# A transformer trunk on one core: layer 0's feed-forward with the context tokens in a pass of their own and the latents' up projection as seven block products

## The reference

```python
def _conv_ffn(u, w_up, conv_w, w_down):
    gate, val = jnp.split(_dwconv3(u @ w_up, conv_w), 2, axis=-1)
    return (jax.nn.silu(gate) * val) @ w_down

for layer in range(DEPTH):            # DEPTH = 2
    mod = silu(c) @ ada_w[layer] + ada_b[layer]      # 6 parts of 1024; mod_c the same from c_ctx
    ...                                              # the layer's mixer, h = h + gt1 * y
    h = h + gt2 * _conv_ffn(_modulate(_rmsnorm(h, norm2[layer]), sh2, sc2), *ffn)
    if not last:
        hc = hc + cgt2 * _conv_ffn(_modulate(_rmsnorm(hc, norm2[layer]), csh2, csc2), *ffn)
```

## Time and profile before

| | |
|---|---|
| median of 3 runs | 3210.61 us (3210.31 to 3213.64) |
| the profiled execution | 3206.37 us, of which the span shown in the trace is 3204.4 us |
| PE busy | 3016.6 us (94%) |
| DVE busy | 1765.9 us (55%) |
| POOL busy | 1015.6 us (32%) |
| ACT busy | 953.6 us (30%) |
| mean granted TensorE clock | 0.974 of full speed |

### The profile page before, as it was taken

One profiled execution on the slowest core, in us unless ns is written; L12 is line 12 of the kernel. 1 busy time (PEld: TensorE's weight loads), 2 busy tenths in 40 slices (PEclk: granted clock), 3 DMA queues, 4 the chain that ended last, 5 costly groups with the idle time before them and its releaser, 6 DMA issues. The chain is left out here.

```text
span 3204.4 us, 67073 instructions
## 1 busy us (share of the span) xinstructions
PE 3016.6 (94%) x28758; PEld 2470.4 (77%) x28758; DVE 1765.9 (55%) x2673; ACT 953.6 (30%) x1800; POOL 1015.6 (32%) x644
## 2 busy tenths in 40 slices
PE   6998999999999999899989889999988899999999
PEld 4655888888888888788867667878767678888887
DVE  4623444555554454722246666777755766666666
ACT  4011221000000000220036566666632433233232
POOL 3212223223333323152311100000004466666664
PEclk9998999999999999999989989999989999999999
DMA  5431011222222221022312011111012111111112
GB/s 236 151 123 37 23 46 46 86 92 92 92 92 92 80 85 40 20 89 81 99 47 63 21 33 29 31 32 34 23 40 92 38 42 66 40 53 66 40 53 79
DMA packets 86541, 210.55 MB, mean 66 GB/s; under 512 B 8434, under 2 KB 44658, under 8 KB 86003
## 3 DMA queue, kind: packets, MB, share of 16 engines
q1 hardware_dynamic: 73442, 157.21, 14.7%
q10 hardware_dynamic: 12816, 49.16, 4.4%
HBM read 185.50 MB, written 20.84 MB: 64 GB/s over the span
## 5 line engine op out<-in xcount | busy, mean ns | idle before, releaser
L155 POOL TENSOR_TENSOR w_hi<-w_raw,zero 128x1024 fp32r<-128x1024 f32 x93 | 177.9, 1913 | 830.0 <-PE ps L167 552.7
L167 PE MATMUL ps<-u_hi,w_hi 128*128 128x512 f32 (+1 forms) x1560 | 395.1, 361 | 3.3 <-DVE ffn_cv L869 2.2
L167 PE MATMUL ps<-u_lo,w_hi 128*128 128x512 f32 (+1 forms) x1560 | 391.4, 358 | 0.0
L167 PE MATMUL ps<-u_hi,w_lo 128*128 128x512 f32 (+1 forms) x1560 | 391.4, 358 | 0.0
L167 PEld LDWEIGHTS ps<-u_hi,w_hi 128*128 128x128 f32 x1560 | 259.6, 188 | 74.2 <-issue 26.6
L167 PEld LDWEIGHTS ps<-u_hi,w_lo 128*128 128x128 f32 x1560 | 259.9, 188 | 46.5
L167 PEld LDWEIGHTS ps<-u_lo,w_hi 128*128 128x128 f32 x1560 | 259.8, 188 | 46.4
L1318 ACT ACTIVATE ffn_cv<-ps,small 128x1280 f32<-128x1280 f32 x44 | 58.6, 1332 | 688.8 <-PE ps L167 680.3
L867 DVE SCALAR_TENSOR_TENSOR ffn_cv<-ps,small,ffn_cv 128x1023 f32<-128x1023 f32 x88 | 77.7, 883 | 307.9 <-ACT ffn_cv L1318 306.4
L158 POOL TENSOR_TENSOR w_lo<-w_raw,w_hi 128x1024 fp32r<-128x1024 f32 x93 | 228.3, 2455 | 7.3
L1697 POOL TENSOR_TENSOR f_w_lo<-h,f_w_hi 128x512 fp32r<-128x512 f32 x92 | 138.4, 1514 | 149.7 <-ACT f_w_hi L1905 149.7
(11 more groups left out here) (443 smaller groups left out, 7040.0 us busy)
## 6 DMA issues: line engine op xcount, KB each, us to landing
w_raw<-in_ffn SPq DMA_DIRECT2D x66, 512.0 KB, 3.4
ada_tile<-in_ada_rows ACTq DMA_DIRECT2D x64, 512.0 KB, 4.0
h<-in_ffn SPq DMA_DIRECT2D x34, 512.0 KB, 4.8
f_w_raw<-in_ffn SPq DMA_DIRECT2D x32, 512.0 KB, 4.0
ada_ring_s<-in_ada SPq DMA_DIRECT2D x22, 512.0 KB, 3.3
w_raw<-in_cd_in SPq DMA_DIRECT2D x20, 512.0 KB, 4.2
z_scratch<-cd_stage ACTq DMA_DIRECT2D x15, 640.0 KB, 5.5
ada_first<-in_ada SPq DMA_DIRECT2D x16, 512.0 KB, 15.5
```

The lines of the kernel that those rows point to most:

```text
L155: pool.tensor_tensor(hi, K.raw[:, raw, :], K.zero[:, 0:1].to_broadcast([P, KT * P]), ALU.add).then_inc(self.hi_done, 1)
L167: mm = pe.matmul(K.ps[:, slot, c, 0:width], wt[:, s, w], x[:, k, at:at + width], start=start and n == 0, stop=stop and n == 2)
```

## The change

`ffn_phase` and `ModRows` go; `split_ffn_phase` takes their place. It has this order:

1. `OutProduct` with `ThreeWayNorm`, whose column sets are context first, then the two latent halves.
2. A pass for the context alone: 66 steps (gate f, value f, down f-1), each 24 products of 256 columns with one whole weight block. ScalarE casts the block (hi, `c_high`), GpSimd subtracts (lo), all 66 of them. Raw blocks have five buffers, hi parts three. Beside it VectorE and ScalarE make the latents' sums of blocks T1 to T4 that the seven products need, one quarter of a step per f, for f = 1 to 16 (`dve_sums`, `act_sums`).
3. The latents: all 22 up items as seven products, 10 down items and the end, as in layer 1, with all weights read a second time. The context's 256 columns of `h` go to memory meanwhile, and their place holds the dot products' operands: one tile buffer. There are two dots in each of the 32 items.
4. `InProduct`: the context comes back, and its squares are summed after the latents' norm steps.

```diff
+class RowDots:
+    DOTS = 48 + 16
+        self.tile = K.h[:, 4:8, SEQ:NT]
+    def act_load(self, act, i):
+        if i:
+            act.wait_ge(self.dots, i)
...
+        act.dma_start(self.tile, self.K.a["ada_rows"][t]...).then_inc(self.tile_in, 16)
+    def dve_dot(self, dve, i):
+        dve.wait_ge(self.tile_in, 16 * (i + 1))
+        dve.scalar_tensor_tensor(self.tile, self.tile, 1.0, self.cond, ALU.mult, ALU.mult,
+                                 accum_out=self.K.mod[:, 1, t, c:c + 1]).then_inc(self.dots, 1)
...
+def split_ffn_phase(K, dram):
+    C_STEPS = [("gate", 0), ("value", 0)]
+    for f in range(1, FT):
+        C_STEPS += [("gate", f), ("value", f), ("down", f - 1)]
+    LOWS, HIGHS, UPS = 5, 3, 3
+    def c_by_dve(n):
+        return False
...
+        # tensor: the context pass
+                    if u >= UPS:
+                        pe.wait_ge(c_conv, u - UPS + 1)
+                            mm = pe.matmul(o, wt[:, w], x[:, k, gap], start=k == 0 and q == 0,
+                                           stop=k == KT - 1 and q == 2)
...
+        # scalar: context pass, value step
+                    act.wait_ge(c_conv, 2 * f + 1)
+                    act.activation(c_gate[:, :], c_gate[:, :], ACT.Silu).then_inc(c_silu, 1)
+                    act.wait_ge(c_done, n + 1)
+                    act.wait_ge(c_ready, f)
+                    act.activation(c_value[:, :], c_up(f, 1), ACT.Identity, scale=tap(1, 1, f)).then_inc(c_centre, 1)
+                if n + HIGHS < C_ALL:
+                    c_high(n + HIGHS)
...
+        # scalar: latents, up item
+                    if t == P7:
+                        keep(n)
+                        if pending is not None:
+                            silu(pending)
+                        rows.act_load(act, a)
+                    if t == P5:
+                        c11(n)
+                        rows.act_load(act, b)
...
+        # vector: latents, up item
+                    if pending is not None:
+                        gated(pending)
+                        rounded(pending)
+                    rows.dve_dot(dve, a)
+                    merge(n, U2)
+                    merge(n, U3)
+                    if pending is not None:
+                        low(pending)
+                    merge(n, C22)
+                    merge(n, C21)
+                    taps(n, 1)
+                    merge(n, C12)
+                    rows.dve_dot(dve, b)
+                    taps(n, 0)
...
 class InProduct:
-        for c in range(3):
+        for c in range(2):
             for m in range(KT):
                 norm.act_square(act, c, m)
...
         for k in range(KT):
             norm.act_hi(act, 1, k)
+        for m in range(KT):
+            norm.act_square(act, 2, m)
         norm.act_root(act, 2)
```

More of the change, by code:

```diff
@@ L873, in conv_taps, with __init__, square_ready @@
     return last
-class InProduct:
[L879 to L883, removed]
+class LateCtxNorm(TokenNorm):
+    def __init__(self, K, added, ctx_back, t_at):
+        super().__init__(K, 2, 3, added, t_at)
+        self.ctx_back = ctx_back
+    def square_ready(self, act, c, m):
+        if c == 2:
+            act.wait_ge(self.ctx_back, 16)
+        else:
+            super().square_ready(act, c, m)
+class InProduct:
+    STEPS = {(1, 5): [0], (1, 6): [1], (1, 7): [2]}
+    LEFT = range(3, KT)
+    def __init__(self, K, end_added, ctx_back):
+        self.K, self.end_added = K, end_added
+        self.st = K.place("cd_stage", [P, 3, NT], F32, at=K.s_at + 16384)
         self.W = Weights(K, "cdin", K.a["cd_in"], ZT)
-        self.norm = TokenNorm(K, 2, 3, end_added, K.s_at + 10240)
+        self.norm = LateCtxNorm(K, end_added, ctx_back, K.s_at + 32768)
         self.done, self.centre, self.ready = K.sem("cdin_done"), K.sem("cdin_centre"), K.sem("cdin_ready")
@@ L931, in pool, with pe_between @@
             W.divide_one(pool, n % 2, self.slot(n), n, n // 2)
[L933 to L937, removed]
+    def pe_between(self, pe, m):
+        if m == 1:
+            self.norm.pe_sums(pe, 0)
+        if m == 4:
             self.norm.pe_spread(pe, 0)
@@ L948, in pe @@
                     mm = product_at(pe, K, m, self.slot(m), K.uhi, K.ulo, k, k, c, at, w, k == 0, k == KT - 1)
+                    if (c, m, k) == (1, 1, 3):
+                        norm.pe_sums(pe, 2)
                 if c == 1:
@@ L1004, in dve_before @@
     def dve_before(self, dve, c, m):
-        if (c, m) in ((1, 3), (2, 7)):
-            self.norm.dve_invert(dve, c - 1)
+        if (c, m) == (1, 3):
+            self.norm.dve_invert(dve, 0)
     def dve_after(self, dve, c, m):
@@ L1019, in dve @@
         K, norm, st, rc = self.K, self.norm, self.st, self.K.S("rconv")
+        for k in self.LEFT:
+            norm.dve_step(dve, 0, k)
+        norm.dve_invert(dve, 1)
         for k in range(KT):
             norm.dve_step(dve, 1, k)
+        for m in range(1, KT):
+            norm.dve_acc(dve, 2, m)
         norm.dve_invert(dve, 2)
@@ L1029, in dve @@
                       rc[:, 24 + m - 6:25 + m - 6], SEGS).then_inc(self.ready, 1)
[L1032 to L1080, removed]
-        gains_of(dve, K, 2)
-        gains_of(dve, K, 3, (0,)).then_inc(self.gains, 1)
-        dve.wait_ge(self.gains, 1)
@@ L4067, in _layout @@
     rows = f["ada_w"][1].T.reshape(48, P, D)
-    arr["ada_rows"] = np.stack([rows[2 * e + r // 2 if r < 4 else 12 + 4 * e + r] for e in range(8) for r in range(8)])
+    arr["ada_rows"] = rows
     arr["cond_rows"] = np.broadcast_to(np.stack([f["c"][0], f["c_ctx"]]), (P, 2, D))
```

1030 lines of the change are left out of this document (741 added, 289 removed).

## The result

The changed kernel takes 3286.45 us in the median of 4 runs (3278.32 to 3287.66), the kernel before 3212.12 (4 runs, 3210.31 to 3219.95). The ratio is 1.022, 95% interval 1.020 to 1.025: slower by 74 us where 27.5 were forecast. The profiled execution has a span of 3285.8 us against 3204.4.

What follows compares the result with a forecast made beforehand. TensorE, busy 904.3 of 907.0 us, was taken to bound the old stretch. Terms -82.0 + 4 + 26 + 66 + 3.5 + 10 = +27.5 us took 3206.4 to 3233.9, plus 4.2 for the median: 3238 us, range 3217 to 3262.

Steps and rivals of the forecast that it cites:

- TensorE's work, -82: Old 907.0 us stretch replaced by 830.8 us of products, last down 5.8 us shorter: -82.0 us if all is fed.
- OutProduct, +4: Context-first OutProduct waits for GpSimd's last weight blocks, up to 4.8 us apart against 2.9 used: +4 us (0 to 6).
- The context pass, +26: VectorE and GpSimd queue for SBUF, 10.2 us per f for 16 f, 8.9 for 6: 216.6 us against 190.1.
- the upper bound: Context pass if taps and a wait for ScalarE line up behind the queue: 13.1 and 11.0 us per f, +86.
- rival B: Slower still: context pass in one chain, nearly 12 us per f, +70; total +75.5, 3286 us; chance 0.13.
- The estimate made from it, 10.6 us and +33: Context pass by the skill page's exclusive lock with whole durations (2.41): 10.6 us per f with sums, +33 us.
- The dots, +66 and +3.5: Latents' part: P4 late in 12 ups, 47.8 us of waits plus 18 of slow clock; hand-over and downs +3.5.
- The end, +10: Last down to InProduct's third block: ScalarE's 11 operations 5 us, the norm's uncovered part as much again; 5 to 15.
- The sum: All terms together: +27.5 us, 3233.9 us profiled, 3238 us as median; forecast's chance 0.48.

Runs made afterwards that it cites:

- lo_vector: Changed kernel with VectorE instead of GpSimd making the context pass's lo parts, all but the first three; 3228.7 us, ratio 1.003 to the kernel before, pass 196.5 us.
- dots_spread: Changed kernel with dot b behind the gate's taps, dot a behind C22 (without `pending`: before U2), and b's load moved in other ups; 3249.9 us, latents' part 654.2.
- pool_busy: lo_vector with GpSimd given two unread 128x512 subtractions per step from the ninth step on; context pass 299.9 us against 196.5.
- cast_ahead: Changed kernel with ScalarE casting the next block before its wait for the gate's taps; ratio 1.016 to the kernel before, context pass 242.1 us.
- lo_halves: Changed kernel with each GpSimd subtraction of the context pass in two halves of 512 columns; ratio 1.017 to the kernel before, pass 248.3 us.
- dots_tiny: Changed kernel with its 64 dots cut to 8 of 1024 columns and 62 of the 64 loads left out; latents' part 666.8 us against 704.
- evac_first: Changed kernel with ScalarE copying InProduct's first block before the root and the context's roundings; last down to third block 74.9 us for 81.4.

## Why the prediction was wrong

- **TensorE's work, -82: right.** Where nothing waits, a context f takes 8.58 to 8.66 us (most of lo_vector's; 8.64 were forecast), and two ups 38.1 (dots_spread; 38.14 were forecast).
- **OutProduct, +4: too large**, +1.4 in both profiles of the changed kernel (118.6 us for 117.2). The second one starts it 3.9 us later, which the forecast had no term for.
- **The context pass, +26: the step that failed.** It was worked out as the time for which the two engines' operations on SBUF fill one queue, 10.1 us per f, and the lower part of the range was taken "because taps can run beside a subtraction". They can, but here they had nothing to run beside. ScalarE's casts stand behind the silu, the silu waits for the taps, and GpSimd waits for the casts: in each round the queue stands empty for 2.9 us of taps and ScalarE's steps, and GpSimd alone for another 2.1 during the sums. The queue's own part was right: 7.5 us for the three operations that each last as long as a subtraction, and 2.1 for the sums, 9.6 where 10.1 were counted. The 2.9 are the very term of the upper bound (four taps of 1.9 and a wait of 1.0) that was put at nothing: 12.5 instead of 10.2 in 16 f is 37 of the missing 42 us.

  That is rival B's chain, and its +70 is the +68.5 measured; I had given it 0.13. That B's total of 3286 meets the median to 1 us is luck: OutProduct, the pass and the dots came 12.4 us below its terms, the end, the rest of InProduct and the part behind it 18.5 above, and the medians differ by 74.3 us where the spans differ by 81.4.

  lo_vector and pool_busy show the exclusion as the cause (-62 to -67 without it, +103 with it restored), cast_ahead and lo_halves that a new order of ScalarE or a shorter subtraction gives back only a part (-16.5 to -22, and -10.3). No run removes the 2.9 us alone; that they are the missing term is read from the timeline. The f without sums took 8.6, as forecast (8.9).

  The Trainium skill's page "SBUF — State Buffer", section "Who interferes with whom", has the second operation blocked until the first ends, whichever starts first; these runs agree (2.40 to 2.63 us beside 2.4). The estimate made from it, 10.6 us and +33, missed for the same reason as mine: it added up durations and left out the time in which neither engine was in the queue.
- **The dots, +66 and +3.5: right in size, in part by errors that offset each other.** The place was right: P4 waits in the 12 ups named, and in f = 0 besides (4.4 us), which was not forecast. The regular wait was 3.0 instead of 3.6, its clock 1.7 instead of 1.5. In f = 2 and 21, where 5.9 were forecast, it was 3.0 too. In all 38.5 us of waits stand where 47.8 were counted, and some 22 of slow clock where 18 were. Inside the regular wait the silu ended where the forecast had it (9.85 us after the item's start, for 9.9). But the load is issued at the silu's start and not behind its end, the tile had landed by 861.1, and what held dot a was VectorE's own multiply and cast: it began 1.3 us earlier than forecast, with no idle time in front of it. Then it took 2.31 us where 1.22 and 0.5 were counted. So the step from the landing to the dot was wrong. Length was not the whole cost, as dots_tiny shows; in other places the same dots hold up no product of the regular ups (dots_spread).
- **The end, +10: too small**, 16.5, above its bound of 15. ScalarE as the releaser of the third block was right (6.5 us, evac_first); the norm's sums and steps in front of InProduct's first blocks cost 10 us and not "as much again" as the 5. (ScalarE's 256-column operation was put at 0.425 to 0.483 us although the row of one beside them had 0.500; the context's take 0.49.)
- **The sum** came out on the right side and at a third of the size. Only 0.13 of the chance stood on B, although the rows already showed the block (2.25 for 1.29) and a GpSimd needed for 84% of the time: that was the misjudgement.

## What to carry to other kernels

When two engines exclude each other, the sum of their operations is a floor and not a forecast: ask who starts them. If both are released by the same third engine, as here, they start together in each round, every short operation of the one pays for a long one of the other, and the time in which the other could have worked alone is lost. Giving the work to the side that is already busier (VectorE made the lo parts at 1.22 us a block for GpSimd's 2.4) can be cheaper than a balance between them. And a side job costs by its place rather than its length: 64 products of 1.2 us and their 4 us loads nearly vanished in gaps that were there anyway (some 13 us stayed, and 3.7 came up behind them), while 8-column stubs in the wrong place cost waits of 0.9 us and more.

## What the runs showed of the hardware

- A cast from fp32 to fp32r with one SBUF input was held up by GpSimd as two-input operations were: 2252 ns against 344 alone.
- VectorE and GpSimd alternated one for one while both had operations on SBUF to do: with subtractions of 1.29 us each sum took 1.77 (0.68 alone), and with subtractions of 2.4 single ones took 2.89. Halving GpSimd's operations (lo_halves) nearly halved each wait, and more operations of VectorE had one.
- VectorE subtracted a 128x1024 block in 1.22 us, GpSimd in 2.4.
- A stage that no one changed varied from 784.6 to 797.2 us between two profiles of one kernel. A difference of 10 us there says nothing about a change.
